# Three edits to the instruction order of the expert stages in a two-layer encoder

## The reference

```
def hier_moe(x, wg, bg, we, be, w1, w3, w2):      # top-1 of 4 groups, top-2 of 8 experts in it
    ...
    def expert_block(args):
        xe, e = args
        hid = jax.nn.silu(xe @ w1[e]) * (xe @ w3[e])
        return hid @ w2[e]
    yb = lax.map(expert_block, (xb, blk_e)).reshape(cap, d)
    out = jax.ops.segment_sum(yb.astype(f32) * buf_gate[:, None], buf_tok, num_segments=t)
```

## Time and profile before

| | us |
|---|---|
| median of 3 runs | 2519.53 (2517.42 to 2526.0) |
| the profiled execution's own time | 2512.4 |
| its span | 2510.6 |
| PE busy | 2322.8 (93%) |
| DVE busy | 1867.1 (74%) |
| ACT busy | 1474.9 (59%) |
| POOL busy | 644.2 (26%) |

### The profile page before, as it was taken

How to read it: one execution, slowest core, us unless ns; L and a number is a source line. 1 busy time by engine, 2 the same in 40 slices (tenths; PEclk the granted TensorE clock), 3 DMA queues, 4 the chain that set the end, 5 groups by cost and what they waited for, 6 DMA issues and landing times. The chain is left out here.

```text
span 2510.6 us, 33111 instructions
## 1 busy us (share of the span) xinstructions
PE 2322.8 (93%) x11266; PEld 1852.2 (74%) x11266; DVE 1867.1 (74%) x2268; ACT 1474.9 (59%) x1814; POOL 644.2 (26%) x430
## 2 busy tenths in 40 slices
PE   8989999889998999999998999998898999999997
PEld 7768877577877777777776877875787777777774
DVE  7838856668468999999994141378768999999993
ACT  6438852322216888888884241267425788888883
POOL 0001100001001354555550000026001354454552
PEclk9989999999998999999999999999998999999999
DMA  5020002110339999999992022012429999999996
GB/s 186 34 69 1 1 17 72 76 34 1 134 140 376 362 395 393 397 394 395 394 369 76 17 101 102 34 48 64 171 93 381 340 412 398 395 399 387 386 350 215
DMA packets 95773, 540.30 MB, mean 215 GB/s; under 512 B 19437, under 2 KB 31374, under 8 KB 70583
## 3 DMA queue, kind: packets, MB, share of 16 engines
q1 hardware_dynamic: 73926, 499.84, 50.4%
q0 software_dynamic: 19008, 33.61, 5.5%
q10 hardware_dynamic: 2736, 5.51, 0.6%
HBM read 519.44 MB, written 55.08 MB: 229 GB/s over the span
## 5 line engine op out<-in xcount | busy, mean ns | idle before, releaser
L2633 DVE TENSOR_TENSOR wL_rest<-ring,wH 128x2048 fp32r<-128x2048 f32 x192 | 431.6, 2281 | 28.5 <-ACT wH L2533 28.5
L2533 ACT CAST wH<-ring 128x2048 fp32r<-128x2048 f32 x192 | 366.6, 1912 | 55.7 <-PE psum L2367 46.2
L2633 DVE TENSOR_TENSOR wL_rest<-xnT,wH 128x2048 fp32r<-128x2048 f32 x128 | 293.0, 2292 | 55.2 <-ACT wH L2533 49.5
L2287 POOL COPY yidx<-slots 128x1 int32 (+1 forms) x64 | 186.1, 2907 | 358.0 <-DMA out<-y,yidx 190.5
L2359 PE MATMUL psum<-wH,xgH 128*128 128x512 f32 x544 | 222.2, 408 | 56.3 <-ACT wH L2533 34.2
L2533 ACT CAST wH<-xnT 128x2048 fp32r<-128x2048 f32 x128 | 243.3, 1905 | 10.8 <-PE psum L2367 9.8
L2359 PE MATMUL psum<-wH,hidH 128*128 128x512 f32 x512 | 206.1, 402 | 19.0 <-ACT wH L2533 13.3
L2361 PE MATMUL psum<-wH,xgL 128*128 128x512 f32 x544 | 215.4, 396 | 0.0
L2361 PE MATMUL psum<-wH,hidL 128*128 128x512 f32 x512 | 199.9, 390 | 0.0
L2359 PEld LDWEIGHTS psum<-wH,xgH 128*128 128x128 f32 x544 | 103.7, 191 | 91.4 <-ACT wH L2533 46.7
L2633 DVE TENSOR_TENSOR wL_rest<-ow,wH 128x2048 fp32r<-128x2048 f32 x64 | 145.9, 2280 | 3.5 <-ACT wH L2533 2.7
(11 more groups left out here) (507 smaller groups left out, 5524.6 us busy)
## 6 DMA issues: line engine op xcount, KB each, us to landing
ring<-in_moe_w SPq DMA_DIRECT2D x92, 2048.0 KB
xnT<-in_moe_w SPq DMA_DIRECT2D x68, 2048.0 KB, 10.3
ow<-in_moe_w SPq DMA_DIRECT2D x34, 2048.0 KB, 9.3
ring<-in_ev_w_in SPq DMA_DIRECT2D x6, 2048.0 KB
ring<-in_od_w_in SPq DMA_DIRECT2D x6, 2048.0 KB
ring<-in_moe_w SPq DMA_DIRECT2D x16, 512.0 KB, 6.3
xn_scratch<-xn_route SPq DMA_DIRECT2D x14, 512.0 KB, 2.6
v_att<-in_x SPq DMA_DIRECT2D x8, 512.0 KB, 4.5
```

Of the source, the lines that this page charges most:

```text
L2287: nc.gpsimd.tensor_copy(yidx[:, b:b + 1], slots[:, bass.ds(at, 1)]).then_inc(yidx_ok, 1)
L2533: nc.scalar.copy(half_of(wH, i, b, c, half), raw(i, b, c, half)).then_inc(w_high, 1)
L2633: return nc.vector.tensor_tensor(out, whole, high.bitcast(F32), ALU.subtract)
```

## The change

Three edits:

- **VectorE, wide stages behind the first:** the remainder of the turned rows goes ahead of `multiply`. Small stages and expert 1 keep `multiply` first.
- **ScalarE, all stages:** the split of up's second half goes ahead of `store_y`.
- **Both:** the turned rows of a wide expert are moved by one operation of 128x1024 over PSUM banks 0 and 1 instead of two of 128x512. So `turned_moves`, the count of these moves, has two to a pair, and ScalarE waits for the last of the eight transposes (`x_hi`) only.

```diff
                 def turned_moves(i, b):
 
-                    if isinstance(i, int) and i == 0:
-                        return 2 * b
-                    return 3 * i + 1 + 2 * b
+                    return 2 * i + b
...
+                    def whole_x():
+                        return psum[:, 0:2, :].rearrange("p b (k t) -> p (b k) t", k=4)
...
-                            for half, turned in ((0, x_lo), (1, x_hi)):
-                                act.wait_ge(turned, e + 1)
-                                nc.scalar.copy(xgH[:, 4 * half:4 * half + 4, :], quarter(half)).then_inc(xh_ok, 1)
+                            act.wait_ge(x_hi, e + 1)
+                            nc.scalar.copy(xgH[:], whole_x()).then_inc(xh_ok, 1)
...
                             split(i, b, 1, 0)
+                            split(i, b, 1, 1)
                             late = not (first(i, b) or second(i, b))
                             if late:
                                 store_y(i - 1, b, *before(i, b), 2)
-                            split(i, b, 1, 1)
                             lower_gate(i, b)
...
-                            for half in range(2):
-                                dve.wait_ge(xh_ok, turned_moves(i, b) + half + 1)
-                                ks = slice(4 * half, 4 * half + 4)
-                                ins = rest(xgL[:, ks, :], quarter(half), xgH[:, ks, :])
-                            ins.then_inc(xl_ok, 1)
+                            dve.wait_ge(xh_ok, turned_moves(i, b) + 1)
+                            rest(xgL[:], whole_x(), xgH[:]).then_inc(xl_ok, 1)
...
                             split(i, b, 0, 0)
-                            if not first(i, b):
+                            if b == 0 and not first(i, b):
+                                move_x(i, b)
+                                multiply(*before(i, b))
+                            elif b:
                                 multiply(*before(i, b))
                                 move_x(i, b)
                             split(i, b, 0, 1)
```

More of the change, by code:

```diff
@@ L2518, in even_x @@
                     def even_x():
-                        return even(psum[:, 0:2, :].rearrange("p b (k t) -> p (b k) t", k=4))
+                        return even(whole_x())
                     @block.scalar
```

## The result

The changed kernel takes 2557.84 us in the median (2548.17 to 2571.58, 4 runs), the kernel before 2518.48 us (2515.93 to 2526.0): ratio 1.0153, 95% interval 1.0108 to 1.0199. It is slower by 39.4 us. The profiled execution took 2548.17 us, the fastest of the four, with a span of 2546.3.

A forecast was written before the change was run, and what follows sets the result against it. Bound: VectorE's `multiply` ahead of the turned rows' remainder, for which TensorE waits. Per layer 11 x 2.55 - 4 x 1.39 = 22.5 us, 45.0 for both; 2512.4 becomes 2557.4, plus 7.1: 2565 us; 8-in-10 range from 2477 to 2480 up to 2600.

The forecast's parts named there:

- Remainder first: Wide stage, VectorE: turned rows' remainder ahead of `multiply` lets TensorE start 1.39 us earlier a pair, 41.7 us in all.
- y later, one operation: ScalarE's y behind up's second half costs nothing; moving turned rows in one operation there differs by at most 0.1 us.
- The new wait: VectorE's row of weight remainders, now without a wait, shuts out GpSimd's copies; GpSimd slips by 7.9 us a pair.
- the very sign that the prediction named: A `yidx` copy ending inside a remainder row without a VectorE wait would refute its reading of when GpSimd gets through.
- (a): Rival: GpSimd keeps up, perhaps getting in where VectorE's loop begins; full gain of 41.7 us, 2478 us; chance 0.25.
- The size: Slips cost 0 to 7.9 us a pair; the middle gives 37.06 us, 2.55 above before, in 11 pairs a layer.
- (c): Rival: GpSimd slips now and then, say in one pair in four; 2490 to 2540 us; chance 0.15.
- (b): Rival: the weights' DMA binds, so 3 pairs a layer go without the gain; 2486 us; chance 0.05.
- (d): Rival: every pair pays for slips, with late gathers that TensorE waits for; 132 us more, 2651 us; chance 0.05.

The follow-up runs named there:

- e5: The changed kernel with both index copies (`yidx` and `gidx`) moved from GpSimd to ScalarE: 2480.0 us, ratio 0.9849.
- e9: The changed kernel with VectorE waiting for its own previous remainder ahead of five of the wide stage's six weight remainders: 2473.52 us, ratio 0.9827.
- e2: The kernel before with only y moved behind both halves of up on ScalarE: 2517.6 us, ratio 0.9992.
- e3: The kernel before with only the turned rows moved by one operation on each of the two engines: 2516.25 us, ratio 1.0004.
- e4: The changed kernel with the small expert's `multiply` one remainder later, behind the wide expert's second one: 2535.55 us, ratio 1.0085.
- e7: The changed kernel with the small expert's `multiply` one remainder later and the wide expert's `multiply` ahead of the small stage's first remainder: 2517.39 us, ratio 1.0003.
- e12: The kernel before with VectorE's same five waits for its own previous remainder in the wide stage: 2517.26 us, ratio 1.0001.
- e11: The changed kernel with only the `gidx` copy moved from GpSimd to ScalarE: 2573.07 us, ratio 1.0204.

## Why the prediction was right

- **Remainder first, gain 1.39 us a pair.** Right. `xgL` takes 1.21 (1.20 taken), the wait of 1.42 us is gone, a clean pair takes 33.05 (33.12). As 30 pairs of this size it was to be worth 41.7 us; with the slips taken away the runs have 37 (e5) and 43 us (e9).
- **y later, one operation: nothing.** Right alone (e2, e3).
- **The new wait.** Right in kind and place: copies of 7.3 to 14.0 us, pairs of unequal length, ScalarE idle ahead of y, TensorE waiting for `xg`. That GpSimd gets through at a wait of VectorE is shown by e9, and in operations out of PSUM by e4 and e7. That it gets through only there is refuted, by the very sign that the prediction named, a `yidx` copy that ends inside a row of remainders with no wait of VectorE. The changed kernel has it (GpSimd's timeline, then VectorE's):

```profile
1196.92 2.05 POOL L2285 COPY yidx<-slots 128x1 int32 x1
```

```profile
1196.64 2.29 DVE L2633 TENSOR_TENSOR wL_rest<-xnT,wH 128x2048 fp32r<-128x2048 f32 x1
1198.85 2.28 DVE L2633 TENSOR_TENSOR wL_rest<-ow,wH 128x2048 fp32r<-128x2048 f32 x1
```

The copy ends at 1198.97, 0.12 behind the start of the second remainder. That one starts 0.08 before the first ends, as remainders in a row do, and ScalarE's split for it had ended 0.44 us earlier (1198.41). This is the seam where VectorE's loop begins, which rival (a) had named. At this seam every copy that was held when it came, 27 of 27 in the twelve traces other than e9's and e12's, ended 0.12 to 0.13 us behind the start.

Most other copies that end inside a row do so where ScalarE had only just ended the split. The one from 2163.00 ends at 2167.71; the next remainder starts at 2167.6, and its split had ended at 2167.53. In the same twelve traces VectorE started a remainder with no gap at 103 seams inside a held copy at most 0.08 us behind the end of its split, and the copy was through at all of them; between 0.08 and 0.095 us it went either way, and at 0.095 to 0.2 us it was through at none of 11. The copy at 2231.23 in the earlier trace rows and the one at 2438.75 in the earlier trace rows are on the two sides of this (0.03 and 0.13 us). That VectorE waits at such a seam is an inference: its start is no later, or by at most 0.02 us, than at a seam where nothing gets through.

This is also where the rule of the Trainium skill, page "SBUF — State Buffer", section "Who interferes with whom", would have misled: by it whoever issues first has the shared port pair for the whole instruction. The copy of 12.52 us at 2116.55, which outlasts the ends of six operations before it gets in, shows that the turn does not go to GpSimd at each instruction's end.

- **The size.** The step that was coarse is "the price is between 0 and 7.9 us a pair. I take the middle", 2.55 more than before in 11 pairs and 1.39 less in 4: a mean pair 1.50 longer. Measured over the 13 pairs: 1.18 and 1.23. It came about otherwise: not every pair pays half a slip, but arrears build up over one to three clean pairs, and the next pays 5.3 to 9.7 at once (13.6 in one). Two terms were missing. The instruction that issues the scatter is held like the copy (15.04 us), which makes GpSimd later; and TensorE's lower clock behind a stall costs 7.0 us in 13 pairs. Against them, fewer pairs paid. That the sum came within 7 us of the median (45.5 forecast, 39.4 measured) is in good part luck: the forecast puts 45.0 us into the experts' parts, where the traces show 23.1.
- **Rivals.** By the number of slips, 8 in 26 pairs, it is near the picture of (c), one pair in four, but at a time beyond its 2540. (a), the full gain, is what the kernel has once GpSimd gets through. (b), the weights' DMA, doesn't bind down to 33.05 us a pair: in e9 the stretch of 13 pairs moves 407 GB/s, against 393 before. (d) had the mechanism of late gathers, not the price.

## What to carry to other kernels

Before closing an idle gap on VectorE, look at who else used it: a small GpSimd copy or DMA issue may have no other way in. Here a back-to-back row of operations with both operands in SBUF shut it out for up to the row's whole length of 14.2 us. Look for GpSimd instructions whose duration varies (0.18 to 14 us for the same 128x1 copy here) and end at VectorE's seams (the places where one operation follows the other), and add up how many of them stand between one landing and the next. The cheapest remedy here was to let VectorE wait for its own last operation, about 0.1 us each time; moving the one copy that stood in that ring to ScalarE did as well.

## What the hardware showed that I had not expected

- An indirect DMA's issue on GpSimd is held by VectorE's row just as a copy is: 1.60 us undisturbed, 15.04 at 2148.52.
- A gap of 0.11 us between two operations of VectorE is enough for the copy that waits (e9). An operation of 0.41 us with one operand in PSUM is not, as a rule: in the changed kernel 11 of the 13 copies that were held over one (`hidL` of the wide stage) did not get through (2124.21, inside the copy of 12.52 us). The other two ended 0.12 us behind its start, and there VectorE's next remainder came 0.66 and 0.78 us after its end. What decides is not shown; three copies in e7 and e11 got through there without such a gap.
- GpSimd got through at every turn of VectorE's loop, though VectorE lost no time there (27 of 27 held copies).
- Some 7 us of standing still cost TensorE more than that: the granted clock is 0.57 on average from 2176 to 2184, in the stall of 7.33 us and behind it, and two products take 0.78 and 0.63 us instead of 0.39.
- Taking work off the engine that is held can make it slower: e11, with one of the four instructions of an expert taken off GpSimd, has the higher median, by 15 us, and longer pairs than the changed kernel (37.01 against 35.84 us).
